# Decoder layer on one core: seven-product steps of the first w_down stage moved in group 0, and two of four weight block sums made by accumulating GpSimd transfers

## The reference

```python
h = rms_norm(x, norm_ffn_g[i])
u = causal_dwconv(h @ w_up[i], ffn_conv_w[i])
u_g, u_v = jnp.split(u, 2, axis=-1)
x = x + (jax.nn.silu(u_g) * u_v) @ w_down[i]
```

## Time and profile before

| | us |
|---|---|
| Time, median of 3 runs (1567.87 to 1569.73) | 1568.05 |
| The profiled execution's own time | 1567.69 |
| Its span | 1565.7 |
| PE, DVE, ACT, POOL busy in the span | 1556.5, 1097.0, 792.9, 33.7 |
| First w_down stage, on PE | 1005.6 to 1133.8 |

### The profile page before, as it was taken

One profiled execution on the slowest core, in us unless ns is written; L12 is line 12 of the kernel. 1 busy time (PEld: TensorE's weight loads), 2 busy tenths in 40 slices (PEclk: granted clock), 3 DMA queues, 4 the chain that ended last, 5 costly groups with the idle time before them and its releaser, 6 DMA issues.

```text
span 1565.7 us, 20901 instructions
## 1 busy us (share of the span) xinstructions
PE 1556.5 (99%) x7694; PEld 1315.2 (84%) x7694; DVE 1097.0 (70%) x1311; ACT 792.9 (51%) x944; POOL 33.7 (2%) x52
## 2 busy tenths in 40 slices
PE   9999999999999999999999999999999999999998
PEld 7878888888888888888888888878888888888887
DVE  5699867776676556655687777788867777755554
ACT  7355454444554444455455555555545555545443
POOL 5000110000000000000000000000000000000000
PEclk9999999999999999999999999999999999999999
DMA  8666655666655666665666656656666666666664
GB/s 271 196 176 190 199 175 170 194 187 190 194 175 179 203 193 193 190 186 174 195 184 186 193 170 200 196 175 214 209 185 188 190 184 178 200 201 189 185 190 151
DMA packets 157479, 297.35 MB, mean 190 GB/s; under 512 B 9655, under 2 KB 14499, under 8 KB 157408
## 3 DMA queue, kind: packets, MB, share of 16 engines
q1 hardware_dynamic: 156896, 296.13, 62.5%
q0 software_dynamic: 480, 0.26, 0.1%
q10 hardware_dynamic: 32, 0.01, 0.0%
HBM read 294.27 MB, written 2.10 MB: 189 GB/s over the span
## 4 chain that ended last, share of the span: by engine, by line
PE 99%; DVE 0%; DMA 0%; ACT 0%; issue 0%; SPq 0%; ACTq 0%
PE psum L537 21%; PE psum L564 18%; PE psum L566 18%; PE psum L565 18%; PE psum L543 11%; PE psum L526 3%; PE psum L527 3%; PE psum L528 3%; PE psum L743 0%; PE psum L689 0%; DMA xtok<-in_x 0%; PE psum L664 0%; PE psum L655 0%; PE psum L652 0%; PE psum L754 0%; PE psum L777 0%
## 5 line engine op out<-in xcount | busy, mean ns | idle before, releaser
L1377 DVE TENSOR_TENSOR w_lo<-raw,w_hi 128x1024 fp32r<-128x1024 f32 x547 | 664.8, 1222 | 383.8 <-ACT w_hi L1015 382.2
L1015 ACT CAST w_hi<-raw 128x1024 fp32r<-128x1024 f32 x546 | 569.9, 1049 | 584.5 <-PE psum L566 391.9
L537 PE MATMUL psum<-h_both,w_hi 128*128 128x512 f32 x1408 | 336.4, 391 | 0.0
L564 PE MATMUL psum<-w_hi,h_both 128*128 128x512 f32 x844 | 332.0, 393 | 0.0
L566 PE MATMUL psum<-w_hi,h_both 128*128 128x512 f32 x844 | 328.7, 389 | 0.0
L565 PE MATMUL psum<-w_lo,h_both 128*128 128x512 f32 x844 | 328.6, 389 | 0.0
L537 PEld LDWEIGHTS psum<-h_both,w_hi 128*128 128x128 f32 x1408 | 258.7, 188 | 50.4 <-DVE rB L1758 0.3
L566 PEld LDWEIGHTS psum<-w_hi,h_both 128*128 128x128 f32 x844 | 158.4, 188 | 33.4
L543 PEld LDWEIGHTS psum<-h_both,w_lo 128*128 128x128 f32 x1408 | 180.6, 191 | 6.9
L564 PEld LDWEIGHTS psum<-w_hi,h_both 128*128 128x128 f32 x844 | 158.5, 188 | 32.7 <-issue 0.3
L565 PEld LDWEIGHTS psum<-w_lo,h_both 128*128 128x128 f32 x844 | 158.6, 188 | 31.9
(11 more groups left out here) (326 smaller groups left out, 1394.8 us busy)
## 6 DMA issues: line engine op xcount, KB each, us to landing
raw<-in_w_up SPq DMA_DIRECT2D x176, 512.0 KB, 3.7
raw<-in_w_gate SPq DMA_DIRECT2D x96, 512.0 KB, 3.7
raw<-in_w_in SPq DMA_DIRECT2D x89, 512.0 KB, 3.7
raw<-in_w_down SPq DMA_DIRECT2D x88, 512.0 KB, 4.4
raw<-in_w_out SPq DMA_DIRECT2D x32, 512.0 KB, 4.5
raw<-in_w_ple_gate SPq DMA_DIRECT2D x32, 512.0 KB, 4.6
raw<-in_w_moba_out SPq DMA_DIRECT2D x16, 512.0 KB, 4.6
raw<-in_w_conv_out SPq DMA_DIRECT2D x8, 512.0 KB, 4.0
```

What stands on the lines that cost most here:

```text
L537: mm = nc.tensor.matmul(wide[part][:, j, :], w_hi[:, c % RING, w], h_both[:, kt + k, :, :].rearrange("p h s -> p (h s)"), start=first and ...
L564: nc.tensor.matmul(o, sh, w_hi[:, c % RING, w], start=first and k == 0, stop=False, skip_group_check=True)
L1015: A.copy(w_hi[:, c % RING, :], raw[:, c % RING, :]).then_inc(chunk_high, 1)
L1377: V.tensor_tensor(w_lo[:, c % RING, :], raw[:, c % RING, :], w_hi[:, c % RING, :].bitcast(F32), ALU.subtract).then_inc(chunk_split, 1)
```

## The change

The positions of the seven-product steps become a table by group, `SEVENS`: 4, 6, 8 and 10 in group 0, and 3, 5, 7 and 9 as before in group 1. `PAIR_OF` is indexed by group and step. The results are taken from PSUM at positions that follow from the last seven-product step (`SEVEN_OUT`, `EIGHT_OUT`): in group 0 that is two chunks later.

Of the four sums of weight blocks DVE keeps two. b12 + b22 is made by a GpSimd transfer that adds b22 from HBM onto b12 in `raw`, once the odd chunk has landed (`third_added`). b11 + b12 is made by a plain SyncE load of b12 into `t_sum[0]` (`t_landed`), issued behind the odd chunk and behind `t_high` and `t_split` of the step before, and a second GpSimd transfer that adds b11 (`first_added`). DVE waits for `first_added` at side 0, and ScalarE for `third_added` ahead of `w_hi` of the odd chunk; the wait for `t_summed` goes behind that `w_hi`.

```diff
--- before.py
+++ after.py
@@ -125,15 +125,19 @@
 MASKED = -1e30
 
 
-SEVEN = (3, 5, 7, 9)
+SEVENS = ((4, 6, 8, 10), (3, 5, 7, 9))
+N_SEVEN = 4
 EIGHT_PAIRS = (0, 2, 4, 6, 8, 9, 10, 11)
 STEPS1 = K1 // 2
 PAIR_OF = {}
-for _n, _s in enumerate(SEVEN):
-    PAIR_OF[_s] = 2 * _n + 1
-for _s, _p in zip([_s for _s in range(STEPS1) if _s not in SEVEN], EIGHT_PAIRS, strict=True):
-    PAIR_OF[_s] = _p
+for _g in range(2):
+    for _n, _s in enumerate(SEVENS[_g]):
+        PAIR_OF[_g, _s] = 2 * _n + 1
+    for _s, _p in zip([_s for _s in range(STEPS1) if _s not in SEVENS[_g]], EIGHT_PAIRS, strict=True):
+        PAIR_OF[_g, _s] = _p
 GROUP1 = 2 * STEPS1
+SEVEN_OUT = {_g * GROUP1 + 2 * SEVENS[_g][-1] + 5: _g for _g in range(2)}
+EIGHT_OUT = {_g * GROUP1 + GROUP1 + 3: _g for _g in range(2)}
 
 
 def trunk(nc, x, p, norm_mix_g, w_in, conv_w, conv_b, conv_ln_g, conv_ln_b, w_conv_out,
@@ -437,8 +442,14 @@
         up(UP1, PAIRS1, 0)
         for k in range(2 * GROUP1):
             g, s, side = place(k)
-            row, col = 2 * PAIR_OF[s] * P, (2 * g + side) * W
+            row, col = 2 * PAIR_OF[g, s] * P, (2 * g + side) * W
             chunk(DOWN1 + k, w_down[0][row:row + 2 * P, col:col + W], 2)
+            if side and s in SEVENS[g]:
+                n_ = N_SEVEN * g + SEVENS[g].index(s)
+                if n_:
+                    sp.wait_ge(t_high, n_)
+                    sp.wait_ge(t_split, n_)
+                sp.dma_start(t_sum[:, 0, :], w_down[0][row:row + P, col:col + W]).then_inc(t_landed, 16)
         up(UP2, PAIRS2, PAIRS1)
         down(DOWN2, K2, K1)
         for g in range(4):
@@ -517,6 +528,17 @@
         rsqrt(1, TT)
         for k, (cols, first) in enumerate(((8, 0), (8, 0), (TT, STAT_CONV), (8, 0), (8, 0), (8, 0), (TT, 0), (TT, 0))):
             rsqrt(2 + k, cols, first)
+            if k == 6:
+                for g in range(2):
+                    for s in SEVENS[g]:
+                        n_ = N_SEVEN * g + SEVENS[g].index(s)
+                        c = DOWN1 + g * GROUP1 + 2 * s + 1
+                        row, col = 2 * PAIR_OF[g, s] * P, 2 * g * W
+                        pool.wait_ge(chunk_landed[c % RING], 16 * (c // RING + 1))
+                        pool.dma_start(raw[:, c % RING, 0:W], w_down[0][row + P:row + 2 * P, col + W:col + 2 * W],
+                                       accum_op=ALU.add).then_inc(third_added, 16)
+                        pool.wait_ge(t_landed, 16 * (n_ + 1))
+                        pool.dma_start(t_sum[:, 0, :], w_down[0][row:row + P, col:col + W], accum_op=ALU.add).then_inc(first_added, 16)
 
 
     @block.tensor
@@ -909,9 +931,9 @@
 
         def seven(g, s):
 
-            u = SEVEN.index(s)
-            n_, (base, own) = len(SEVEN) * g + u, banks(g)
-            first, last = u == 0, u == len(SEVEN) - 1
+            u = SEVENS[g].index(s)
+            n_, (base, own) = N_SEVEN * g + u, banks(g)
+            first, last = u == 0, u == N_SEVEN - 1
             c = DOWN1 + g * GROUP1 + 2 * s
             one, two = slice(0, W), slice(W, 2 * W)
             low, high_ = slice(0, P), slice(P, S)
@@ -1279,14 +1301,15 @@
         def down_high(k):
 
             g, s, side = place(k)
-            if k >= 2 * GROUP1 or s not in SEVEN:
+            if g > 1 or s not in SEVENS[g]:
                 high(DOWN1 + k)
                 return
-            n_ = len(SEVEN) * g + SEVEN.index(s)
+            n_ = N_SEVEN * g + SEVENS[g].index(s)
+            if side:
+                act.wait_ge(third_added, 16 * (n_ + 1))
+            high(DOWN1 + k)
             if side:
                 act.wait_ge(t_summed, n_ + 1)
-            high(DOWN1 + k)
-            if side:
                 if n_:
                     act.wait_ge(t_used, n_)
                 A.copy(t_hi[:], t_sum[:]).then_inc(t_high, 1)
@@ -1294,23 +1317,22 @@
         def seven_out(g):
 
             own = banks(g)[1]
-            act.wait_ge(t_used, len(SEVEN) * (g + 1))
+            act.wait_ge(t_used, N_SEVEN * (g + 1))
             if g:
                 act.wait_ge(x_step, 3 * g)
             A.copy(p1m[:, 0, :], psum[:, own, :])
             A.mul(q7m[:, 0:W], psum[:, own + 3, :], -1.0)
             A.copy(q7m[:, W:2 * W], psum[:, own + 3, :]).then_inc(seven_copied, 1)
 
-        with act.Fori(0, len(SEVEN)) as i:
+        with act.Fori(0, N_SEVEN) as i:
             up_pair(i, UP1, 0, U_F, True)
-        for i in range(len(SEVEN), PAIRS1):
+        for i in range(N_SEVEN, PAIRS1):
             up_pair(i, UP1, 0, U_F, False, down_high if i == PAIRS1 - 1 else None)
         for k in range(12, 2 * GROUP1 + 12):
             down_high(k)
-            g = k // GROUP1
-            if k == g * GROUP1 + GROUP1 - 1:
-                earlier()
-                seven_out(g)
+            if k in SEVEN_OUT:
+                earlier()
+                seven_out(SEVEN_OUT[k])
         up(UP2, PAIRS2, PAIRS1, U_F + PAIRS1)
         n = K2 // 2
         for c in range(DOWN2 + 12, END + 4):
@@ -1854,22 +1876,18 @@
 
             g, s, side = place(k)
             c = DOWN1 + k
-            if k >= 2 * GROUP1 or s not in SEVEN:
+            if g > 1 or s not in SEVENS[g]:
                 split(c)
                 return
-            n_ = len(SEVEN) * g + SEVEN.index(s)
+            n_ = N_SEVEN * g + SEVENS[g].index(s)
             if not side:
-                b11, b21 = (raw[:, c % RING, h * W:(h + 1) * W] for h in range(2))
-                b12, b22 = (raw[:, (c + 1) % RING, h * W:(h + 1) * W] for h in range(2))
+                b21, b22 = (raw[:, (c + h) % RING, W:2 * W] for h in range(2))
                 dve.wait_ge(chunk_landed[c % RING], 16 * (c // RING + 1))
                 dve.wait_ge(chunk_landed[(c + 1) % RING], 16 * ((c + 1) // RING + 1))
                 if n_:
                     dve.wait_ge(t_high, n_)
                     dve.wait_ge(t_split, n_)
-                V.tensor_tensor(t_sum[:, 0, :], b11, b12, ALU.add).then_inc(t_step, 1)
-                V.tensor_tensor(b12, b12, b22, ALU.add)
-                t_steps[0] += 1
-                dve.wait_ge(t_step, t_steps[0])
+                dve.wait_ge(first_added, 16 * (n_ + 1))
                 V.tensor_tensor(t_sum[:, 1, :], t_sum[:, 0, :], b22, ALU.add).then_inc(t_step, 1)
                 t_steps[0] += 1
                 dve.wait_ge(t_step, t_steps[0])
@@ -1920,23 +1938,26 @@
             v = xtok[:, :, col:col + 2 * W]
             V.tensor_tensor(v, v, psum[:, base:base + 4, :].rearrange("p (t b) n -> p t (b n)", t=TT), ALU.add).then_inc(taken[base // 4], 1)
 
-        with dve.Fori(0, len(SEVEN)) as i:
+        with dve.Fori(0, N_SEVEN) as i:
             up_pair(i, UP1, NG_UP1, 0, U_F, d0, True)
-        for i in range(len(SEVEN), PAIRS1):
+        for i in range(N_SEVEN, PAIRS1):
             up_pair(i, UP1, NG_UP1, 0, U_F, d0, False, down_split if i == PAIRS1 - 1 else None)
         d0 += 2 * PAIRS1
         for k in range(12, 2 * GROUP1 + 12):
             down_split(k)
-            g, r = divmod(k, GROUP1)
-            if r == GROUP1 - 1:
-                earlier()
-                seven_banks(g)
-            if g and r < 3:
-                earlier()
-                seven_adds(g - 1, r)
-            if g and r == 3:
-                earlier()
-                eight_banks(g - 1)
+            if k in SEVEN_OUT:
+                earlier()
+                seven_banks(SEVEN_OUT[k])
+            if k - 1 in SEVEN_OUT:
+                earlier()
+                seven_adds(SEVEN_OUT[k - 1], 0)
+                seven_adds(SEVEN_OUT[k - 1], 1)
+            if k - 2 in SEVEN_OUT:
+                earlier()
+                seven_adds(SEVEN_OUT[k - 2], 2)
+            if k in EIGHT_OUT:
+                earlier()
+                eight_banks(EIGHT_OUT[k])
         V.memset(upg[:, :, 0:2], 0.0)
         V.memset(upv[:, :, 0:2], 0.0).then_inc(pads_ready, 1)
         dve.wait_ge(pads_ready, 1)
```

More of the change, by code:

```diff
@@ L234, in trunk @@
     f_lo = ar("f_lo", [P, K1, S], 44.5, F32R)
-    form_hi = ar("form_hi", [P, 3 * len(SEVEN), P], 68.5, F32R)
-    form_lo = ar("form_lo", [P, 3 * len(SEVEN), P], 74.5, F32R)
+    form_hi = ar("form_hi", [P, 3 * N_SEVEN, P], 68.5, F32R)
+    form_lo = ar("form_lo", [P, 3 * N_SEVEN, P], 74.5, F32R)
     form = ar("form", [P, 3, P], 84.5)
@@ L304, in trunk @@
     t_summed, t_step, t_high, t_split, t_used = sem("t_summed"), sem("t_step"), sem("t_high"), sem("t_split"), sem("t_used")
+    t_landed, first_added, third_added = sem("t_landed"), sem("first_added"), sem("third_added")
     seven_copied, seven_step, x_step, pads_ready = sem("seven_copied"), sem("seven_step"), sem("x_step"), sem("pads_ready")
@@ L893, in eight @@
         def eight(g, s):
-            base, pair_ = banks(g)[0], PAIR_OF[s]
+            base, pair_ = banks(g)[0], PAIR_OF[g, s]
             if g == 0:
@@ L951, in _ @@
             for s in range(STEPS1):
-                if s in SEVEN:
+                if s in SEVENS[g]:
                     seven(g, s)
@@ L1897, in seven_banks @@
```

(2 more changed lines are left out.)

## The result

| | before | after |
|---|---|---|
| Time, median | 1567.96 us (4 runs) | 1613.3 us (4 runs) |
| Profiled execution, its span | 1567.69, 1565.7 | 1612.58, 1610.8 |
| First w_down stage, first matmul to the next stage's first | 1005.60 to 1133.60 | 1005.99 to 1178.76 |

The ratio is 1.0287, with a 95% interval of 1.0275 to 1.0299: 45 us slower. The stage took 128.00 us and takes 172.77, so 44.8 of the profiled executions' 44.9 us arose in it.

The account below looks back on a forecast made before the run. PE (TensorE), busy 99%, bounds the kernel, with a buffer loop of 10.17 us right behind its 10.20. Terms -2.8 + 1.45 + 2.9 + 31.2 = +32.8 us on the median of 1568.05 gave 1601 us, range 1580 to 1630.

Parts of the forecast that it names:

- The stall at 1023 us: Opening step 3 of group 0, PE waiting ahead of chunk 8: moving the seven-product steps removes it, -2.8 us.
- The loop: Split of an odd chunk to the next such split: 9.9 + A, 15.4 us against PE's 10.20; 5.2 lost, six times.
- A: GpSimd's second transfer, into t_sum: time to landing, taken as 5.5 us; each microsecond moves the sum by about 8.
- load of `t_sum`: SyncE's plain load in the loop: issued 1.95 us after the split, landing after 4.0 us.
- rival 1: Short transfers on GpSimd's queue: A = 2.1, loop 12.0, +8, 1576 us; chance of A under 3: 0.08.
- high end of 10 us: Upper value for A: two 256 KB transfers one behind the other, each as long as two plain ones at worst.
- The first step of each group: First seven-product step, starting from PE's lead: 1.45 us lost in group 0 and 2.9 in group 1.
- The clock: Within slow accumulation (A 8 to 10, 1621 to 1637 us, chance 0.18): PE waits over 7 us may drop it to 1.2 GHz.
- 32.8: Whole kernel: forecast slowdown in us, summed from -2.8, 1.45, 2.9 and 31.2.
- the range: Whole kernel's time: 1580 to 1630 us for 8 in 10.
- signs: In the loop: odd splits 15.4 us apart, PE idle near 5 us before six chunks, DVE's add released by a DMA.
- other-side rival: At DVE's wait for first_added: transfers landing within 0.3 us stay hidden, -2.8, 1565 us; chance 0.06, partial forms included.

Follow-up runs that it names:

- the shift alone: Changed kernel with all four sums made by DVE and the waits of the kernel before, no transfers added; 1567.1 us, ratio 0.9989 to before.
- first-sum-only kernel: Changed kernel with b12 + b22 made by DVE and only b11 + b12 by load and accumulating transfer; 1600.6 us, ratio 1.0211 to before.
- unwaited kernel: Changed kernel with all four sums on DVE, the same loads and accumulating transfers going to two buffers that nothing reads; 1567.85 us, ratio 0.9999 to before.
- prefetched: Changed kernel with only b11 + b12 made by transfer, one seven-product step ahead in alternating buffers, b12 + b22 on DVE; 1566.0 us, ratio 0.9986 to before.
- third-sum-only kernel: Changed kernel with b11 + b12 on DVE, no load into t_sum, only b12 + b22 by accumulating transfer; 1593.5 us, ratio 1.0161 to before.

## Why the prediction was right, by its steps

**The stall at 1023 us**, -2.8: the shift alone took 2.1 us off the stage and 1.4 to 1.8 off the time. The step is right. I claimed for that kernel that nothing would take its place, and two waits of 0.3 and 0.2 us did.

**The loop** 9.9 + A: the chain that it adds up is the one in the trace, its size was 15.4 and is 16.6. One loop, term by term (the first line is not in the sum, since the second holds it):

| | predicted | measured (1111.86 on) |
|---|---|---|
| split to GpSimd's first transfer | 5.25 | 5.30 |
| split to GpSimd's second transfer | 6.05 | 7.18 |
| to DVE's add | 5.6 (A 5.5 and 0.1) | 5.95 |
| adds and two splits | 3.76 | 3.69 |
| sum | 15.4 | 16.82 |

The mis-sized term is the load of `t_sum`. I took 4.0 us from the earlier trace rows; it took 5.0 at the median and 5.2 here, and GpSimd's transfer started 0.3 us after its landing. In the first-sum-only kernel, without GpSimd's first transfer, the load lands in 4.0 us again, as the row has it, and A falls to 5.1. I had priced the load from transfers that had no such neighbour. What it is of the first transfer that lengthens the load stays open: with a quarter of its bytes the load still took 4.9 us, with plain loads 5.0, but in the unwaited kernel, where a chunk and that transfer are on their way beside it as well, only 4.2. Six loops of 1.2 us are 7.2 us.

**A**: 5.5 predicted, 5.8 measured. The Trainium skill's fit ("DMA: Bandwidth & Descriptors", Anatomy of one DMA — SWDGE path) gave 2.6 us for 256 KB as an estimate. Here it doesn't hold: the plain loads of that size on this queue took 4.3 and 5.0 us to landing. (Reckoned as in rival 1, that A would have made the sum +11, not +10.) The rival of short transfers fell with it; no landing of 256 KB on this queue was under 3.6 us, and by the estimate from a quarter of the bytes 3.1 us would be there for none. What the Trainium skill says in "Collectives: The Full Stack" (The bandwidth ceiling) of the second source read points the right way: adding cost 1.2 to 1.5 us, though no run here shows that the second read is the reason. My high end of 10 us doesn't follow from the words beside it: two transfers, each as long as two plain ones of 4.0 us, would be 16.

**The first step of each group**: 1.45 and 2.9 predicted. PE's gap ahead of chunk 8 is 2.1 us (matmuls 2.33 apart), ahead of chunk 30 it is 3.3.

**The clock** stood among the rivals with its effect hidden in the loop, which held. But I tied its fall to waits of over 7 us, and it came after waits of 3.1 to 6.0; and that it has an unhidden tail behind a group wasn't in the sum.

The account: 32.8 + 7.2 (loops) + 0.65 and 0.4 (first steps) + 1.9 (tail of group 1) = 43.0 us, against 44.9 between the profiled executions. Of the 1.9 us left, up to 1 can be the tail of group 0; the rest is not accounted for. So the mechanism is as forecast, and the cost came out 12 us too low (44.9 for 32.8), with nearly every miss of a term on the same side. That the time lies in the range (1580 to 1630) is in part luck: the range was drawn for A, which was off by only 0.3 us, and the larger misses were in terms that I had taken as certain.

**What I named as signs:** splits of odd chunks 15.4 apart (16.6), PE idle near 5 us before chunks 12, 16, 20, 34, 38 and 42 (4.2 to 6.0), DVE's add released by a DMA into `t_sum` (all eight): all there. The other-side rival needed 0.3 us to landing, and the shortest median landing of these transfers in any kernel was 3.8 us.

## What to carry to other kernels

Before work is moved to a DMA, find the loop of buffers it would lie in, and write its period as a sum: here load, sums, splits, 10.17 us against PE's 10.20. An engine's 1.2 us saved in such a loop is nothing beside a landing of 4 to 6 us put into it, and the same transfer issued a step ahead, into a buffer of its own, cost nothing here. Price a transfer from a row in which its neighbours were on their way too, and before changing how a stall's work is done, try only moving it: that alone took the stall here.

## What the runs showed of the hardware

- An accumulating transfer of 128 rows of 2 KB from GpSimd's queue took at the median 5.8 to 6.7 us from issue to landing in kernels with two of them in each seven-product step. With one in each it took 4.9 to 5.5 (prefetched), 5.1 (onto `t_sum`) and 6.1 (onto `raw`). Plain ones took 4.3 and 5.0, accumulating ones of 512-byte rows 3.8 and 5.1. The one onto `raw` was the longer wherever both kinds of place were compared in the changed kernel, with plain loads and with a quarter of the bytes; why wasn't tried. Issuing one keeps GpSimd busy 0.87 us, a plain one 0.55.
- Such transfers with nobody waiting lengthened the chunk loads from 4.8 us (shift only) to 5.3 at the median and left DVE's and ScalarE's instructions as long as they were (`w_lo` 1.22 us, `w_hi` 1.05).
- In the changed kernel matmuls of 512 columns started 0.43 us apart, 5 to 8 of them, after PE's waits of 3.1 to 6.0 us, at the clock's lower level of 1.2 GHz; after the wait of 1.95 us ahead of chunk 8 none did. The length of the wait alone doesn't tell: in the third-sum-only kernel two waits of 2.47 us were followed by seven slow matmuls (from 1031.69) and by none (from 1129.86), and in the first-sum-only kernel one of 1.93 us by seven and one of 3.33 us by none.
